# Narrower products in the last layer of a two-block transformer kernel: columns 14 to 271, and 16 to 271, in place of 0 to 271

## Chip, cores and metric

The kernel runs on one core of one Trainium2 chip. The metric is the device time of one launch in microseconds (us), the median of several runs. Inputs and outputs are float32.

## What is computed

The reference runs a first block (two layers on 256 latent tokens, with 256 context tokens beside them in the first layer) and feeds its output to a second block. The change touches the second block alone:

```python
N_META, DEPTH, CONV_W, PAD = 16, 2, 3, 128
h = concat([zeros(PAD - N_META), meta, x])          # 112 empty rows, 16 meta tokens, 256 tokens
for li in range(DEPTH):
    h = h + mixer(rms_norm(h, norm_mix_g[li]), ...)
    h = h + conv_ffn(rms_norm(h, norm_ffn_g[li]), ...)
h = rms_norm(h, norm_final_g)
return h[:, PAD:]                                   # the meta tokens are not returned

def mixer(hn, ...):
    proj = hn @ w_in                                # 13 groups of 1024 columns
    o_ret, o_hg, o_da = retention(...), hgrn2(...), diff_attention(...)   # mix tokens; two of them end in "* silu(gate)"
    y_b = [o @ w_branch[n] for n, o in enumerate((o_ret, o_hg, o_da))]
    return sum(sigmoid(mg[n]) * y_b[n]) @ w_out

def conv_ffn(hn, ...):
    u = hn @ w_ffn_in                               # width 5632
    c = conv_b + sum(conv_w[j] * up[:, j:j + l] for j in range(CONV_W))   # token t reads t-2, t-1, t
    gate, val = split(c); return (silu(gate) * val) @ w_ffn_out
```

The kernel holds the 16 meta tokens and the 256 tokens as columns 0 to 15 and 16 to 271 (`T2` = 272). The 112 empty rows are never computed. After the last layer's mixers have read keys and values of every token, no returned value depends on columns 0 to 13 any more. Columns 14 and 15 are read once more by the convolution of column 16.

## The kernel before

Everything is laid out feature-major: 128 features on the partitions, tokens along the free axis. Each product of activations with a weight matrix is done in float32 accuracy by three products of rounded parts (type float32r): high weight by high activation, high weight by low activation, low weight by high activation. They are lines 1861, 1862 and 1863, in `gemm_unit` of the TensorE program.

A weight matrix is cut into **units** of 256 output columns, a unit into **chunks** of up to four blocks of 128 input features. The tiles are these:

- `raw`, `high`, `low`: four slots of one chunk each, 128x1024. SP loads a chunk into `raw` (line 1683), ScalarE rounds it to `high` (`split_high`, line 1951), VectorE subtracts to get `low` (`split_low`, line 2136).
- `NHh`, `NHl`: high and low part of the normed activations of the second block, `OH`, `OL` those of a mixer's output, `G2H`, `G2L` those of the feed-forward's hidden layer.
- `PS`: the eight PSUM banks. Unit u writes banks 0 and 1 or 2 and 3 in turn, so that one unit's results are read out while the next is multiplied.

A unit with 1024 input features is 2 chunks x 2 output tiles x 4 blocks x 3 = 48 products. A unit of the feed-forward's output matrix has 2816 input features (6 chunks) and 22 x 2 x 3 = 132 products.

`gemm_steps` writes down the list of steps once, and every engine walks the same list. In each layer of the second block it is: stores, gate (8 or 4 units) for each of three mixers n = 0, 1, 2, then for each mixer its own attention-like part (`ret_pe`, `hg_pe`, `da_pe`), the merge gate (`mgate`, 4 units) and the branch matrix (`branch`, 4 units). Mixer 0 (retention) and mixer 1 (hgrn2) have a `gate` step of 4 units each, mixer 2 has none. Then come the output matrix (`add`, 4 units), the feed-forward's input matrix with the convolution in its epilogue (`conv`, 22 units) and its output matrix (`add` with 6 chunks, 4 units). The first two units of every `mgate` step are issued early, from within the mixer's own part, by `early_chunk` (lines 1788 to 1790) or `early_piece` (lines 1804 to 1806).

No scheduler is involved. The order on each engine is that of the program text; engines wait for each other by semaphores: `s_low` (a chunk is ready to multiply), `s_chunk` (a chunk is multiplied, its slot is free), `s_free` (a unit's banks are read out). The epilogues stand at lines 2296 to 2347 (VectorE) and 1999 to 2043 (ScalarE). For a `conv` unit they are: two scaled copies on ScalarE (line 2022), four multiply-adds of the shifted taps on VectorE (line 2331), a sigmoid on ScalarE (line 2043) and two products on VectorE (lines 2343, 2347). Each of them takes all 272 columns.

`keep_busy` issues products with a matrix of ones that nobody reads (line 529), to fill known waits of TensorE.

Of the kernel before, what the change touches and what calls it, by code (L numbers as in the profile page):

```python
# [33 lines left out]
D = 1024  # L34
KT = D // P
F = 2816
FT = F // P
SEQ = 256
CTX = 256
N_META = 16  # L40
T1 = SEQ + CTX
T2 = N_META + SEQ
DEPTH = 2
# [4 lines left out]
DEEP = ((0, 4), (4, 4), (8, 4), (12, 4), (16, 3), (19, 3))  # L48
# [96 lines left out]
    return out  # L145


def gemm_steps(w):


    steps = []

    def add(name, units, src, layer=0, t0=0, T=SEQ, kch=SHALLOW, unroll=False):
        steps.append(dict(name=name, units=units, src=src, layer=layer, t0=t0, T=T, kch=kch, unroll=unroll))

    def plain(ap, col0=0):
        v = ap.rearrange("(k p) n -> p k n", p=P)

        def src(u, k0, nk):

            n0 = (nk + 1) // 2
            return [(v[:, k0 + a:k0 + b, bass.ds(col0 + UW * u, UW)], slice(a, b), slice(0, UW))
                    for a, b in ((0, n0), (n0, nk))]
        return src

    def paired(ap, first, second):

        v = ap.rearrange("(k p) n -> p k n", p=P)

        def src(u, k0, nk):  # L170
            return [(v[:, k0:k0 + nk, bass.ds(at + P * u, P)], slice(0, nk), slice(x * P, (x + 1) * P))
                    for x, at in enumerate((first, second))]
        return src

    for layer in range(DEPTH):
        for r in range(3):
            T = T1 if (layer, r) == (0, 0) else SEQ
            if r != 1:
                half = 0 if r == 0 else 1
                add("glu", FT, paired(w["ffn_w_in"][layer, half], 0, F), layer, T=T, unroll=(layer, r) == (0, 0))  # L180
                add("res", 4, plain(w["ffn_w_out"][layer, half]), layer, T=T, kch=DEEP)
                steps[-1]["r"] = r
            elif layer == 0:
                add("v", 4, plain(w["na_w_qkv"][0], 2 * D), layer, T=T1)
                add("k", 4, plain(w["na_w_qkv"][0], D), layer, T=T1)
                steps[-1]["pairs"], steps[-1]["halves"] = {1: 0, 2: 1, 3: 2}, {u: u for u in range(4)}
                add("q", 4, plain(w["na_w_qkv"][0], 0), layer)
                steps[-1]["pairs"], steps[-1]["halves"] = {u: 3 + u for u in range(4)}, {u: 4 + u for u in range(4)}
                add("res", 4, plain(w["na_w_out"][0]), layer)
                steps[-1]["r"] = r  # L190
            else:
                add("cgate", 8, paired(w["sc_w_in"][0], D, 2 * D), layer)
                add("bgate", 4, plain(w["sc_w_in"][0], 0), layer)
                add("res", 4, plain(w["sc_w_out"][0]), layer)
                steps[-1]["r"] = r
            steps[-1]["norm"] = True
    for layer in range(DEPTH):
        w_in = w["w_in_2"][layer]
        for n, kinds in enumerate(((("store", 4, 0, 0), ("store", 4, 1024, 8), ("gate", 4, 2048, 16)),
                                   (("store", 4, 3072, 0), ("forget", 4, 4096, 8), ("store", 4, 5120, 24),  # L200
                                    ("gate", 4, 6144, 32)),
                                   (("store", 4, 9216, 16), ("store", 8, 7168, 0)))):
            for kind, units, at, tile in kinds:
                add(kind, units, plain(w_in, at), layer, T=T2, unroll=True)
                steps[-1]["tile"] = tile
                steps[-1]["at"] = at
                steps[-1]["after_rms"] = at == 0
                steps[-1]["rope"] = {0: {1: (0, 1), 2: (2, 3), 3: (4, 5)}, 1024: {0: (6, 7)},
                                     7168: {u: (2 * u - 2, 2 * u - 1) for u in range(1, 8)}}.get(at, {})
                steps[-1]["values"] = {2048: 0, 6144: 1, 7168: 2}.get(at)  # L210
            steps[-1]["mixer"] = n
            add("mgate", 4, plain(w_in, 10240 + n * D), layer, T=T2)
            steps[-1]["n"] = n
            steps[-1]["begun"] = 2
            add("branch", 4, plain(w["w_branch_2"][layer, n]), layer, T=T2)
            steps[-1]["n"] = n
        add("add", 4, plain(w["w_out_2"][layer]), layer, T=T2)
        steps[-1]["rms"] = ("ffn_g", layer)
        add("conv", FT, paired(w["w_ffn_in_2"][layer], 0, F), layer, T=T2)
        steps[-1]["after_rms"] = True  # L220
        add("add", 4, plain(w["w_ffn_out_2"][layer]), layer, T=T2, kch=DEEP)
        steps[-1]["rms"] = ("mix_g", layer + 1) if layer + 1 < DEPTH else ("final_g", 0)
    U, S = 0, 0
    for s in steps:
        s["U0"], s["S0"] = U, S
        U += s["units"]
        S += s["units"] * len(s["kch"])
    return steps, S
# [23 lines left out]
def two_block_kernel(nc, w, tokens, meta, cols_d, const1_d, const2_d, rpb_d, rpb_skew, out_d):  # L252
    steps, n_chunks = gemm_steps(w)
    ctx = ExitStack()
    with ctx:
# [89 lines left out]
        NHh = B.take("NHh", [P, KT, T2], F32R)  # L345
        nhl_at = B.at
        NHl = B.take("NHl", [P, KT, T2], F32R)
# [29 lines left out]
        PS = ctx.enter_context(nc.psum_tensor("PS", [P, 8, PW], F32))  # L377
# [139 lines left out]
        def bank(p, j, n=1):  # L517
            return PS[:, 2 * p + j:2 * p + j + n, :]
# [1210 lines left out]
        def _(pe):  # L1729
# [47 lines left out]
            def early_chunk(s, x):  # L1777

                u, c = divmod(x, 2)
                S, b = s["S0"] + x, early_bank(s["n"], u)  # L1780
                pe.wait_ge(s_low, S + 5)
                if c == 0:
                    pe.wait_ge(s_free, s["U0"] + u + (2 if s["n"] == 1 else 1))
                for j in range(2):
                    for k in range(4):
                        wh, wl = high[:, x, k, j * P:(j + 1) * P], low[:, x, k, j * P:(j + 1) * P]
                        xh, xl = NHh[:, 4 * c + k, :], NHl[:, 4 * c + k, :]
                        nc.tensor.matmul(PS[:, b + j, 0:T2], wh, xh, start=(c == 0 and k == 0), stop=False)
                        nc.tensor.matmul(PS[:, b + j, 0:T2], wh, xl, start=False, stop=False)
                        last = nc.tensor.matmul(PS[:, b + j, 0:T2], wl, xh, start=False, stop=(c == 1 and k == 3))  # L1790
                last.then_inc(s_chunk, 1)

            def early_piece(s, i):

                f, c = divmod(i, 2)
                u, j = divmod(f, 2)
                x = 2 * u + c
                pe.wait_ge(s_low, s["S0"] + x + 5)
                if c == 0 and f:
                    pe.wait_ge(s_fill, 4 * s["layer"] + f)  # L1800
                for k in range(4):
                    wh, wl = high[:, x, k, j * P:(j + 1) * P], low[:, x, k, j * P:(j + 1) * P]
                    xh, xl = NHh[:, 4 * c + k, :], NHl[:, 4 * c + k, :]
                    nc.tensor.matmul(PS[:, 6, 0:T2], wh, xh, start=(c == 0 and k == 0), stop=False)  # L1804
                    nc.tensor.matmul(PS[:, 6, 0:T2], wh, xl, start=False, stop=False)  # L1805
                    last = nc.tensor.matmul(PS[:, 6, 0:T2], wl, xh, start=False, stop=(c == 1 and k == 3))  # L1806
                if j:
                    last.then_inc(s_chunk, 1)
                elif c:
                    last.then_inc(s_filled, 1)  # L1810

            for n_step, s in enumerate(steps):
                name, T, t0 = s["name"], s["T"], s["t0"]
# [3 lines left out]
                if name in ("glu", "q", "k", "v", "cgate"):  # L1817
                    mh, ml = XH, XL
                elif name == "res":
                    mh, ml = (XH, XL) if (s["layer"] == 0 and s["r"] == 1) else (GH, GL)  # L1820
                elif name in ("store", "gate", "forget", "mgate", "conv"):
                    mh, ml = NHh, NHl
# [22 lines left out]
                def gemm_unit(u, p, S, slot0):  # L1845
                    kch = s["kch"]
                    for c, (k0, nk) in enumerate(kch):
# [5 lines left out]
                                pe.wait_ge(s_oln, half_first(s["layer"], 2) + 2)  # L1853
                        slot = (slot0 + c) % NSLOT
                        for j in range(2):
                            out = bank(p, j)[:, :, 0:T].rearrange("p a n -> p (a n)")
                            for k in range(nk):
                                wh = high[:, slot, k, j * P:(j + 1) * P]
                                wl = low[:, slot, k, j * P:(j + 1) * P]
                                xh, xl = mh[:, k0 + k, t0:t0 + T], ml[:, k0 + k, t0:t0 + T]  # L1860
                                nc.tensor.matmul(out, wh, xh, start=(k0 + k == 0), stop=False)  # L1861
                                nc.tensor.matmul(out, wh, xl, start=False, stop=False)  # L1862
                                last = nc.tensor.matmul(out, wl, xh, start=False,  # L1863
                                                        stop=(c == len(kch) - 1 and k == nk - 1))
# [704 lines left out]
```

## Time and profile before

| | us |
|---|---|
| median of 3 runs | 3172.04 (3171.92 to 3173.32) |
| the profiled execution, its own time | 3167.65 |
| span of its records | 3165.8 |
| last layer of the second block, within the span | about 2342 to 3166 |
| TensorE busy, share of the span | 95% |
| VectorE, ScalarE, GpSimd busy | 54%, 42%, 13% |
| mean granted TensorE clock | 0.976 |

The profile gives the start of each TensorE instruction exactly and models its end, so a product of 272 columns shows as 0.29 us although the next starts 0.126 us after it. The distance from start to start is therefore what a product costs in a dense stretch. In a window of the view by stretches, the count of TensorE includes the two products that still run when the window opens; the distance is the window's length divided by the count less 2.

### The profile page before, as it was taken

What the parts mean: (1) busy time and instruction counts of PE and PEld (TensorE: products, weight loads), DVE (VectorE), ACT (ScalarE), POOL (GpSimd) and SP (SyncE); (2) the same over time, 40 slices, a digit from 0 to 9 for tenths busy, and PEclk for the clock granted to TensorE, in tenths of its full rate; (3) what the DMA queues carried; (4) which work ended last, traced back from release to release, by engine and by line L of the source; (5) the groups of instructions that cost most, each with busy time, mean ns of one, the idle gap of its engine ahead of it and who ended that gap; (6) DMA issues with size and microseconds to landing.
All of it is one profiled execution on the core that took longest, in us unless ns stands there. A gap on an engine that the chain in (4) does not pass through costs nothing. (4 is left out here: it accounts for less than half of the span.)

```text
span 3165.8 us, 54076 instructions
## 1 busy us (share of the span) xinstructions
PE 2992.5 (95%) x21052; PEld 2702.8 (85%) x21052; DVE 1713.8 (54%) x2476; ACT 1341.5 (42%) x1838; POOL 408.5 (13%) x306
## 2 busy tenths in 40 slices
PE   5999998988999999999999999899999998999998
PEld 2667765666999999899899889799999997988998
DVE  2223324365555556555545755657754576565784
ACT  1222213135544434443454443556544453445563
POOL 2111000122111210121100210101110012020110
PEclk8999999999999999999999989999999998999999
DMA  8986354731555654465445315245543540533553
GB/s 295 282 251 185 121 160 125 218 95 54 160 181 148 182 180 149 143 180 181 134 127 164 110 40 174 81 134 152 173 154 120 167 153 14 161 93 116 147 172 124
DMA packets 586161, 474.88 MB, mean 150 GB/s; under 512 B 28720, under 2 KB 547888, under 8 KB 585664
## 3 DMA queue, kind: packets, MB, share of 16 engines
q1 hardware_dynamic: 584464, 460.44, 47.6%
q0 software_dynamic: 1520, 11.95, 1.2%
q8 instruction: 127, 2.08, 0.3%
q14 instruction: 50, 0.41, 0.0%
HBM read 471.23 MB, written 4.72 MB: 150 GB/s over the span
## 5 line engine op out<-in xcount | busy, mean ns | idle before, releaser
L2136 DVE TENSOR_TENSOR low<-raw,high 128x1024 fp32r<-128x1024 f32 (+1 forms) x744 | 913.1, 1231 | 837.3 <-ACT high L1951 829.2
L1951 ACT CAST high<-raw 128x1024 fp32r<-128x1024 f32 (+1 forms) x744 | 767.9, 1033 | 1102.3 <-PE PS L1863 807.6
L1861 PE MATMUL PS<-NHh,high 128*128 128x272 f32 x2304 | 672.9, 292 | 12.4 <-issue 4.7
L1863 PE MATMUL PS<-NHh,low 128*128 128x272 f32 x2304 | 666.2, 289 | 0.0
L1862 PE MATMUL PS<-NHl,high 128*128 128x272 f32 x2304 | 664.4, 288 | 0.0
L1861 PE MATMUL PS<-XH,high 128*128 128x256 f32 (+1 forms) x1856 | 587.4, 316 | 28.4 <-issue 14.4
L1862 PE MATMUL PS<-XL,high 128*128 128x256 f32 (+1 forms) x1856 | 579.4, 312 | 0.0
L1863 PE MATMUL PS<-XH,low 128*128 128x256 f32 (+1 forms) x1856 | 579.1, 312 | 0.0
L1861 PEld LDWEIGHTS PS<-NHh,high 128*128 128x128 f32 x2304 | 433.8, 188 | 17.2 <-issue 14.8
L1862 PEld LDWEIGHTS PS<-NHl,high 128*128 128x128 f32 x2304 | 434.0, 188 | 0.8
L1863 PEld LDWEIGHTS PS<-NHh,low 128*128 128x128 f32 x2304 | 433.5, 188 | 0.0
L1861 PEld LDWEIGHTS PS<-XH,high 128*128 128x128 f32 x1856 | 356.7, 192 | 79.1 <-issue 58.9
L1863 PEld LDWEIGHTS PS<-XH,low 128*128 128x128 f32 x1856 | 356.5, 192 | 20.1
L1862 PEld LDWEIGHTS PS<-XL,high 128*128 128x128 f32 x1856 | 356.8, 192 | 17.8
L1861 PE MATMUL PS<-GH,high 128*128 128x256 f32 (+1 forms) x768 | 238.8, 311 | 0.8 <-POOL GL L2461 0.8
L1863 PE MATMUL PS<-GH,low 128*128 128x256 f32 (+1 forms) x768 | 236.2, 308 | 0.0
L1862 PE MATMUL PS<-GL,high 128*128 128x256 f32 (+1 forms) x768 | 236.1, 307 | 0.0
L2461 POOL TENSOR_TENSOR GL<-SG,GH 128x256 f32 (+1 forms) x92 | 122.3, 1329 | 722.8 <-ACT GH L2036 628.8
L1861 PEld LDWEIGHTS PS<-GH,high 128*128 128x128 f32 x768 | 146.6, 191 | 26.4 <-issue 20.3
L1863 PEld LDWEIGHTS PS<-GH,low 128*128 128x128 f32 x768 | 146.7, 191 | 7.2
L1862 PEld LDWEIGHTS PS<-GL,high 128*128 128x128 f32 x768 | 146.7, 191 | 6.2
L2353 DVE TENSOR_TENSOR SG<-SG,PS 128x256 f32<-128x256 f32 (+1 forms) x88 | 42.9, 487 | 155.7 <-ACT SG L1999 155.7
(315 smaller groups left out, 4109.3 us busy)
## 6 DMA issues: line engine op xcount, KB each, us to landing
raw<-w_in_dram SPq DMA_DIRECT2D x416, 256.0 KB, 3.0
raw<-ffn_w_in_dram SPq DMA_DIRECT2D x352, 256.0 KB, 3.2
part<-ada_w_dram SPq DMA_DIRECT2D x184, 256.0 KB, 3.9
raw<-w_ffn_in_dram SPq DMA_DIRECT2D x176, 256.0 KB, 3.2
raw<-ffn_w_out_dram SPq DMA_DIRECT2D x160, 256.0 KB, 3.1
raw<-w_branch_dram SPq DMA_DIRECT2D x96, 256.0 KB, 3.3
raw<-w_ffn_out_dram SPq DMA_DIRECT2D x80, 256.0 KB, 3.0
part_sg<-ada_w_dram SPq DMA_DIRECT2D x48, 256.0 KB, 3.0
```

The lines of the kernel that those rows point to most:

```text
L1861: nc.tensor.matmul(out, wh, xh, start=(k0 + k == 0), stop=False)
L1862: nc.tensor.matmul(out, wh, xl, start=False, stop=False)
L1863: last = nc.tensor.matmul(out, wl, xh, start=False, stop=(c == len(kch) - 1 and k == nk - 1))
L1951: nc.scalar.copy(high[:, slot, 0:nk, :], raw[:, slot, 0:nk, :]).then_inc(s_high, 1)
L2136: nc.vector.tensor_tensor(low[:, slot, 0:nk, :], raw[:, slot, 0:nk, :], high[:, slot, 0:nk, :].bitcast(F32), ALU.subtract).then_inc(s_low, 1)
L2353: nc.vector.tensor_tensor(sg, sg, bank(p, 0)[:, :, 0:T], ALU.mult).then_inc(s_mid, 1)
L2461: nc.gpsimd.tensor_tensor(out, x, h.bitcast(F32), ALU.subtract).then_inc(s_hl, 1)
```

## The change

The column range of a step, `t0` to `T`, existed but `t0` was always 0. Now `needed(layer)` gives 0 for the first layer of the second block and 14 (`N_META - 2`) for the last. The steps `gate`, `mgate`, `branch`, both `add` steps and `conv` of the last layer get it; for the second `add` (the feed-forward's output) it is 16. The moving operand and the PSUM output of their products begin at that column. Weights, loads, splits, waits and epilogues stay: the epilogues of VectorE and ScalarE still read all 272 columns of the banks, of which the first 14 or 16 now hold what an earlier product left. Each engine has the same instructions in the same order as before.

```diff
+def needed(layer):
+    return 0 if layer + 1 < DEPTH else N_META - 2
...
+                if kind == "gate":
+                    steps[-1]["t0"] = needed(layer)
...
-            add("mgate", 4, plain(w_in, 10240 + n * D), layer, T=T2)
+            add("mgate", 4, plain(w_in, 10240 + n * D), layer, t0=needed(layer), T=T2)
...
-            add("branch", 4, plain(w["w_branch_2"][layer, n]), layer, T=T2)
+            add("branch", 4, plain(w["w_branch_2"][layer, n]), layer, t0=needed(layer), T=T2)
...
-        add("add", 4, plain(w["w_out_2"][layer]), layer, T=T2)
+        add("add", 4, plain(w["w_out_2"][layer]), layer, t0=needed(layer), T=T2)
...
-        add("conv", FT, paired(w["w_ffn_in_2"][layer], 0, F), layer, T=T2)
+        add("conv", FT, paired(w["w_ffn_in_2"][layer], 0, F), layer, t0=needed(layer), T=T2)
...
-        add("add", 4, plain(w["w_ffn_out_2"][layer]), layer, T=T2, kch=DEEP)
+        add("add", 4, plain(w["w_ffn_out_2"][layer]), layer, t0=needed(layer) and N_META, T=T2, kch=DEEP)
...
-                            out = bank(p, j)[:, :, 0:T].rearrange("p a n -> p (a n)")
+                            out = bank(p, j)[:, :, t0:T].rearrange("p a n -> p (a n)")
...
-                                xh, xl = mh[:, k0 + k, t0:t0 + T], ml[:, k0 + k, t0:t0 + T]
+                                xh, xl = mh[:, k0 + k, t0:T], ml[:, k0 + k, t0:T]
```

`early_chunk` and `early_piece` get the same slices, `s["t0"]:T2`, for both operands and the output.

## Rows read from the trace of the kernel before

**Rows 1.** The page: span, TensorE, VectorE and its clock in 40 slices.

```profile
span 3165.8 us, 54076 instructions
...
PE 2992.5 (95%) x21052; PEld 2702.8 (85%) x21052; DVE 1713.8 (54%) x2476; ACT 1341.5 (42%) x1838; POOL 408.5 (13%) x306
...
PEclk8999999999999999999999989999999998999999
```

**Rows 2.** The chain that ended last, from 2940 us on: start, us, what.

```profile
2955.23 0.36 PE PS L1861
3151.76 0.73 DVE H L2321
```

**Rows 3.** Stretches: length, then PE busy (count), PEld, DVE, ACT, POOL, clock, DMA.

```profile
2958.00:3082.00 124.00, 124.00 (x985) 124.00 (x985) 101.31 (x163) 79.72 (x124) 20.98 (x20) 1.00 0.58 171
3090.00:3150.00 60.00, 60.00 (x481) 60.00 (x481) 24.86 (x25) 21.17 (x24) 6.09 (x6) 1.00 0.44 137
1130.00:1190.00 60.00, 60.00 (x502) 60.00 (x501) 28.98 (x30) 22.37 (x23) 6.19 (x6) 1.00 0.60 181
300.00:350.00 50.00, 50.00 (x222) 41.42 (x221) 16.17 (x17) 13.87 (x17) 6.93 (x5) 1.00 0.24 74
2706.30:2709.40 3.10, 3.10 (x15) 3.10 (x15) 2.83 (x3) 2.60 (x4) 0.00 (x0) 0.50 0.59 185
```

**Rows 4.** Waits of TensorE from 2342 us on: us in total, times, longest.

```profile
PE PS L1139 <- DVE AM L1363: 2.9, 1, 2.9
...
PE PS L1861 <- DVE NHl L1667: 2.3, 3, 1.5
PE PS L1861 <- DVEq L2305: 2.1, 1, 2.1
...
PE PS L1788 <- DVE MG L2300: 1.6, 1, 1.6
...
PE PS L1861 <- DVE MG L2300: 1.1, 1, 1.1
```

**Rows 5.** Timeline around the second merge gate's end: start, length, instruction, idle before.

```profile
2703.39 0.29 PE L1863 MATMUL PS<-NHh,low 128*128 128x272 f32 x1
2703.64 1.28 ACT L2008 ACT_TABLE_LOAD   x1
...
2704.93 0.62 ACT L2008 ACTIVATE GR<-PS 128x544 f32<-128x544 f32 x1
...
2705.79 0.36 PE L1861 MATMUL PS<-OH,high 128*128 128x272 f32 x1 [2.11 <-DVEq L2305]
```

**Rows 6.** Timeline of VectorE and TensorE in hgrn2's gate.

```profile
2577.05 5.03 DVE L1323 TENSOR_TENSOR_SCAN MI<-con,MI 128x272 f32<-128x272 f32 x8
...
2583.34 0.70 DVE L2300 TENSOR_TENSOR MG<-MG,PS 128x544 f32<-128x544 f32 x1
...
2584.19 0.36 PE L1861 MATMUL PS<-NHh,high 128*128 128x272 f32 x1 [1.08 <-DVE MG L2300]
```

**Rows 7.** Timeline of VectorE, one unit of the last `conv` step.

```profile
2995.71 2.19 DVE L2331 SCALAR_TENSOR_TENSOR CB<-PS,cols,CB 128x271 f32<-128x271 f32 x4 [0.62 <-ACT CB L2022]
2997.82 1.22 DVE L2136 TENSOR_TENSOR low<-raw,high 128x1024 fp32r<-128x1024 f32 x1
2998.95 0.43 DVE L2343 TENSOR_TENSOR SG<-SG,CB 128x272 f32<-128x272 f32 x1
2999.51 0.44 DVE L2347 TENSOR_TENSOR SG<-SG,CB 128x272 f32<-128x272 f32 x1
2999.87 1.22 DVE L2136 TENSOR_TENSOR low<-raw,high 128x1024 fp32r<-128x1024 f32 x1
```

**Rows 8.** Stretch of the last layer's stores of mixer 2, columns as in rows 3.

```profile
2779.00:2811.00 32.00, 32.00 (x243) 31.37 (x242) 20.82 (x34) 9.47 (x10) 11.72 (x10) 1.00 0.49 152
```

More of the change, by code:

```diff
@@ L1786, in early_chunk @@
                         wh, wl = high[:, x, k, j * P:(j + 1) * P], low[:, x, k, j * P:(j + 1) * P]
[L1787 to L1790, printed above, removed]
+                        xh, xl = NHh[:, 4 * c + k, s["t0"]:T2], NHl[:, 4 * c + k, s["t0"]:T2]
+                        out = PS[:, b + j, s["t0"]:T2]
+                        nc.tensor.matmul(out, wh, xh, start=(c == 0 and k == 0), stop=False)
+                        nc.tensor.matmul(out, wh, xl, start=False, stop=False)
+                        last = nc.tensor.matmul(out, wl, xh, start=False, stop=(c == 1 and k == 3))
                 last.then_inc(s_chunk, 1)
@@ L1802, in early_piece @@
                     wh, wl = high[:, x, k, j * P:(j + 1) * P], low[:, x, k, j * P:(j + 1) * P]
[L1803 to L1806, printed above, removed]
+                    xh, xl = NHh[:, 4 * c + k, s["t0"]:T2], NHl[:, 4 * c + k, s["t0"]:T2]
+                    out = PS[:, 6, s["t0"]:T2]
+                    nc.tensor.matmul(out, wh, xh, start=(c == 0 and k == 0), stop=False)
+                    nc.tensor.matmul(out, wh, xl, start=False, stop=False)
+                    last = nc.tensor.matmul(out, wl, xh, start=False, stop=(c == 1 and k == 3))
                 if j:
```

## The prediction
> **What bounds the kernel now.** I read the page first. TensorE is busy for 95% of a span of 3165.8 us, and its clock is full nearly everywhere [rows 1]. Busy time alone doesn't say that TensorE sets the end, since its ends are modelled. So the chain of work that ended last comes next: from 2955.23 us, where the last layer's `conv` step gets going, to 3151.76 us it is nothing but products of lines 1861 to 1863, and only then come the last addition and the final norm [rows 2]. Third come the waits of TensorE in the last layer: the largest one of a product that the change touches is 2.1 us, and all that touch such a product are in rows 4. TensorE is the bound of this layer, with short breaks inside the mixers. So what counts is what a product costs from start to start, and at which breaks a shorter product only waits longer.
>
> **The cost of a product by its width.** The view by stretches gives it, each window's length divided by its count less 2 [rows 3]. In the last `conv` step 272 columns cost 124.0 / 983 = 126.1 ns. In the feed-forward's output step, also 272 columns, they cost 60.0 / 479 = 125.3 ns. In the first block's output step of 1130 to 1190 us, 256 columns cost 60.0 / 500 = 120.0 ns. In the window at 300 us, 512 columns cost 50.0 / 220 = 227.3 ns. Between 256 and 272 a column is worth 6.1 / 16 = 0.38 ns, between 272 and 512 it is 101.2 / 240 = 0.42 ns. So the width is paid for, on top of a fixed part of some 13 ns. The changed products have 258 columns, two more than a width that the trace shows: 120.0 + 2 x 0.38 = **120.8 ns**, 5.3 ns less than before. Bounds: not below the 120.0 ns of 256 columns, and not above the 126.1 ns of today unless the new start column costs something (a rival, below). I take 120.8, since the nearest row is two columns away.
>
> The Trainium skill, "TensorE: Matmul & The Clock Gate", section on the back-to-back issue gap, has the distance at full clock as N / 2.4 + 2.5 ns. The trace differs on the fixed part (13 ns, not 2.5) and nearly agrees on the slope. By the page's slope a product saves 14 / 2.4 = 5.8 ns, and the sum below would be 18.7 us instead of 16.6.
>
> **The change, part by part.** Products of 258 columns: `gate` 8 units, `mgate` 12, `branch` 12, the output matrix 4, `conv` 22, together 58 units of 48, or 2784 products. Products of 256 columns: 4 units of 132, or 528.
>
> *conv, 1056 products.* The stretch is dense for all of its 124 us [rows 3]. What must keep up is VectorE: in one unit, 2995.71 to the last row's end, it has 2.19 + 1.22 + 0.43 + 0.44 + 1.22 = 5.50 us of work, with some overlap, and before it 0.62 us of idle time that ended with a ScalarE result [rows 7]. A unit now takes 48 x 126.1 = 6.05 us and will take 5.80 us. VectorE's idle time shrinks from 0.62 to about 0.37 us and stays above nothing. Its result is needed only when the unit after next begins, so a delay of a few tenths is covered by a whole unit. DMA is busy at 0.58 and the 256-wide stretch ran at 0.60 [rows 3], so loads can follow. Full gain: 1056 x 5.3 = 5.6 us.
>
> *Feed-forward output, 528 products.* Dense too, VectorE busy 24.9 of 60 us [rows 3]. 125.3 - 120.0 = 5.3 ns each: 2.8 us, all on the chain [rows 2].
>
> *The other 1728 products.* Most stand back to back with TensorE's next work. At two places the gain is swallowed:
> - The second merge gate's units 2 and 3 (96 products) end at 2703.4, and the branch product starts only at 2705.79, when a sigmoid of ScalarE (2704.93) is out. That one stood behind a table load and the casts of the mixer's output, none of which waits for those 96 [rows 5]. Shorter products lengthen this wait: gain nothing.
> - In hgrn2's gate, VectorE spends 2577.05 to 2583.34 on the running sums and only then frees the banks of unit 0; TensorE waits for it until 2584.19 [rows 6]. Units 0 and 1 (96 products) end earlier for nothing, but for a little of unit 0 that lets VectorE begin sooner. I count nothing.
>
> The rest keeps its gain. The waits for `L2300` before an early piece and for `L1363` after it [rows 4] follow the end of products and move with them; those for `L1667` come after the norm, and move as well. The third merge gate is followed by no wait in rows 4. So 1728 - 192 = 1536 products x 5.3 = 8.1 us.
>
> Half clock: 2706.3 to 2709.4 ran at 0.50 (1.2 of 2.4 GHz), after the break before it, and held 15 products [rows 3, 5]. At half clock 14 columns are worth twice as much, 13 x 5.8 = 0.1 us more. The break before it gets 0.5 us longer, so this stretch stays.
>
> Nothing is removed on VectorE, ScalarE, GpSimd, SP or the DMA queues, so nothing else is gained.
>
> **Sum:** 5.6 + 8.1 + 0.1 + 2.8 = **16.6 us**. The profiled execution took 3167.65 us by its own time (span 3165.8), 4.4 us under the median of 3172.04. The sum is a difference within that execution, and I take it off both: 3151.0 for such an execution, **3155.4 us** for the median, a gain of 0.5%.
>
> **Rivals.**
>
> *B. The start at column 14 takes back what the width gives.* Columns 0, 16 or 128 begin at a multiple of 64 bytes in their row, column 14 at byte 56, and the touched 258 columns reach into as many 64-byte pieces (17) as the 272 did. All widths in rows 3 start at column 0, so no row shows an uneven start. If reads go by such pieces, only the 528 products from column 16 gain: 2.8 us, 3169.2. Against it: nothing seen, only lack of a row.
>
> *C. The weight load sets most of the pace.* Every product has a load of its own. The 256 to 512 rows speak against it, with 0.38 and 0.42 ns a column [rows 3]. As a mechanism here, 258 would be near a floor, and the gain would be small: at a third of the slope, 2592 x 1.8 + 528 x 2.1 = 5.8 us, 3166.2. The Trainium skill, same page and section, gives for pairs of load and product 81 ns at 128 columns and 131 ns at 512, a slope of 0.13 ns; by this rule the time would be that of C, but the trace's 227.3 ns at 512 contradicts it.
>
> *D. Another engine holds the `conv` step.* If VectorE and ScalarE, which still take 272 columns, kept the unit at 6.05 us, the 5.6 us of `conv` would be lost: 11.0 us gained, 3161.0. For it: 5.50 us of work in 5.80. Against it: the 0.62 us of idle time, and a whole unit of cover [rows 7].
>
> *E. Slower: the uneven start makes reading slower.* Place: the moving operand and the PSUM output of 2592 products. It outweighs the 2.8 us of the feed-forward's output from 1.1 ns a product above today's 126.1, and costs 0.2% from 3.5 ns. The nearest dearer row at full clock is the stores' stretch, 32.0 / 241 = 132.8 ns, other work and small breaks included [rows 8]. At that price it is 2592 x 6.7 - 2.8 = 14.6 us slower, 3186.6. For it there is only that no row shows column 14; against it, that a read of fewer columns would have to cost more than a read of all.
>
> That the change doesn't do what it says can be left out: the diff narrows each product, and count and order stay.
>
> **How the numbers follow.** A (the forecast) 0.80, B 0.07, C 0.03, D 0.06, E 0.04. Within A: at 120.0 ns and with the 192 swallowed products counted, 2784 x 6.1 + 2.8 = 19.8 us; at a price halfway to today's, 2592 x 3.05 + 2.8 = 10.7 us. A stretch of half clock more or less costs some 1.4 us (15 products counted in 3.1 us where full clock holds 3.1 / 0.126 + 2 = 26.6) [rows 3]. A's own range is thus 3151 to 3162. With D inside and 1 us for a half-clock stretch at either end, **3150 to 3163**; it leaves out B, C, E and the tails of A. A measurement of this kernel can tell about 0.2% (6.3 us) from no change. Faster: A and D, 0.86. Within: B and C, 0.10. Slower: E, 0.04.
>
> **What would show it.** In the changed profile: the `conv` window shows about 120.8 ns a product and no wait on VectorE or ScalarE; the feed-forward's output shows 120.0. The wait before the second branch product grows from 2.1 to about 2.6 us, that in hgrn2's gate from 1.1 to about 1.6. The last addition of the page's chain starts about 16.6 us sooner. The forecast is wrong if the 258-column products show 126 ns or more (B, E) while those from column 16 show 120, if both barely move (C), or if a wait of a microsecond appears in the `conv` step (D).

## The result, and the profile after

The changed kernel takes 3147.35 us (median of 6 runs, 3140.8 to 3151.08), the kernel before 3172.68 us in the same comparison (3170.8 to 3173.86). The ratio is 0.9921, with a 95% interval of 0.9912 to 0.9931: 25.1 us less, between 21.9 and 27.9. The forecast was 16.6 us less, with a range that ended at 3150 us. So direction and place were right, and the gain was half as large again as forecast.

The page of the changed kernel, with its execution of 3140.8 us:

```profile
span 3139.0 us, 54076 instructions
...
PE 2966.2 (94%) x21052; PEld 2677.4 (85%) x21052; DVE 1714.8 (55%) x2476; ACT 1343.3 (43%) x1838; POOL 408.3 (13%) x306
...
PEclk8999999999999999999999989999999999999999
```

TensorE is busy 26.3 us less than in [rows 1], VectorE as long as before. Lines are 7 to 9 higher than before: 1861 to 1863 are now 1870 to 1872. The chain that ended last, from 2915 us on (start, us, what), has the same links as in [rows 2]:

```profile
2938.93 0.36 PE PS L1870
3124.94 0.73 DVE H L2330
```

The cost of a product comes from the same view as in [rows 3], columns as there, the window's length divided by the count less 2:

```profile
2945.00:3060.00 115.00, 115.00 (x963) 115.00 (x962) 99.54 (x161) 76.82 (x121) 21.02 (x20) 1.00 0.62 181
3065.00:3122.00 57.00, 57.00 (x486) 57.00 (x485) 26.89 (x28) 21.64 (x25) 6.11 (x6) 1.00 0.47 150
2467.00:2488.00 21.00, 21.00 (x179) 21.00 (x178) 11.39 (x11) 8.17 (x8) 0.00 (x0) 1.00 0.62 190
1125.00:1185.00 60.00, 60.00 (x502) 60.00 (x502) 29.84 (x31) 22.33 (x24) 6.59 (x6) 1.00 0.60 183
```

That is 115.0 / 961 = 119.7 ns in the `conv` step, 57.0 / 484 = 117.8 ns in the feed-forward's output, 118.6 ns in the first branch step (118.9 as the mean of its start distances), and still 120.0 ns for 256 columns in the first block. The forecast had 120.8, 120.0 and 120.8 for the first three. The same width of 256 columns thus costs 120.0 ns in one place and 117.8 in another. That is what the experiments are about.

Where the time went, by the first and last start of each step in both traces: from the last layer's first product to the end of the span it was 817.1 us and is 793.8, so 23.3 us less. The `conv` step has 6.6 of it (133.65 to 127.06), the feed-forward's output 3.9 (65.98 to 62.07), everything else in the layer 12.8. Another 3.6 us of the 26.8 between these two spans had come before the layer began, where nothing was changed; that part is chance.

The waits of TensorE from 2338 us on (us in total, times, longest):

```profile
PE PS L1870 <- DVE NHl L1674: 2.4, 3, 1.5
...
PE PS L1870 <- DVEq L2314: 2.3, 1, 2.3
...
PE PS L1796 <- DVE MG L2309: 1.6, 1, 1.6
PE PS L1870 <- DVE MG L2309: 1.5, 1, 1.5
```

They answer to [rows 4]. The wait before the second branch product grew from 2.1 to 2.3 us and the one in hgrn2's gate from 1.08 to 1.54; the other two moved by no more than 0.1. The timeline of hgrn2's gate, start and length, shows the second one, as in [rows 6]:

```profile
2575.58 0.71 DVE L2309 TENSOR_TENSOR MG<-MG,PS 128x544 f32<-128x544 f32 x1
...
2576.43 0.36 PE L1870 MATMUL PS<-NHh,high 128*128 128x258 f32 x1 [1.54 <-DVE MG L2309]
```

One stretch of half clock is gone. It had lain at the start of the second branch step, whose 192 products run from 2705.79 to 2731.45 us in the kernel before (first fence) and from 2696.32 to 2719.26 us in the changed one (second fence; columns as in [rows 3]):

```profile
2705.79:2731.45 25.66, 25.66 (x191) 25.66 (x192) 16.23 (x16) 10.46 (x11) 0.00 (x0) 0.93 0.67 205
```

```profile
2696.32:2719.26 22.94, 22.94 (x192) 22.94 (x192) 16.16 (x16) 10.47 (x11) 0.00 (x0) 1.00 0.71 218
```

The step is 2.7 us shorter, of which the width explains 192 x 6.4 ns = 1.2 us (126.1 to 119.7 ns in this step) and the clock, 1.00 in place of 0.93, the other 1.5.

### The profile page after: what moved, and what is told of

It is laid out like the page before. It is cut to its first block and busy times, and to the rows that moved or that the text cites. A ratio compares the mean times of both kernels' runs of the same rounds, so it can differ in the third digit from the quotient of the medians.

```text
span 3139.0 us, 54076 instructions
## 1 busy us (share of the span) xinstructions
PE 2966.2 (94%) x21052; PEld 2677.4 (85%) x21052; DVE 1714.8 (55%) x2476; ACT 1343.3 (43%) x1838; POOL 408.3 (13%) x306
## 5 line engine op out<-in xcount | busy, mean ns | idle before, releaser
L1870 PE MATMUL PS<-NHh,high 128*128 128x272 f32 (+1 forms) x2304 | 669.0, 290 | 13.1 <-DVE NHl L1674 4.7
L1872 PE MATMUL PS<-NHh,low 128*128 128x272 f32 (+1 forms) x2304 | 661.5, 287 | 0.0
L1871 PE MATMUL PS<-NHl,high 128*128 128x272 f32 (+1 forms) x2304 | 660.2, 287 | 0.0
```

The costliest lines, as they stand in the source:

```text
L1872: last = nc.tensor.matmul(out, wl, xh, start=False, stop=(c == len(kch) - 1 and k == nk - 1))
```

## The experiments

All start from the changed kernel unless said otherwise. Ratios are to the kernel before. The runs from column 0, with the table of widths and with 128 columns leave out columns that the result needs; they measure cost alone.

**Start column or width?** Operands and outputs of the same widths, but from column 0:

```diff
-                            out = bank(p, j)[:, :, t0:T].rearrange("p a n -> p (a n)")
+                            out = bank(p, j)[:, :, 0:T - t0].rearrange("p a n -> p (a n)")
-                                xh, xl = mh[:, k0 + k, t0:T], ml[:, k0 + k, t0:T]
+                                xh, xl = mh[:, k0 + k, 0:T - t0], ml[:, k0 + k, 0:T - t0]
```

The same slices stand in `early_chunk` and `early_piece`.

> Same widths as the change, but from column 0: products read and write columns 0 to 257 (0 to 255 in the feed-forward's output), so the last columns of the last layer are left out. In the changed kernel a product of 258 columns cost 118.9 ns (119.7 in the conv step) and one of 256 columns 117.8 ns, not the forecast 120.8 and 120.0. Theory W (the width alone, with a fixed part of some 11 ns wherever tiles lie 1088 bytes apart): the same distances within 0.5 ns, and a time within 3 us of the change's 3147. Rival S (the start at byte 56 or 64 of a row is what makes products cheaper): 258 columns come back to 120.8, 256 to 120.0, time about 3155.

Measured: 3148.86 us, ratio 0.9927 (0.9910 to 0.9943). `conv` had 115.0 / 960 = 119.8 ns, the feed-forward's output 58.0 / 492 = 117.9 ns, the three branch steps 119.7 ns. With column 14 those had 118.9, 119.7 and 118.9. So the width does nearly all, and the uneven start costs nothing. Whether it gives the 0.8 ns in two of the steps is not shown: with column 14 the same step had 118.9 in one run and 119.7 in another. Rival S fell.

**Where the row starts.** All tiles of the first block 64 bytes later:

```diff
-        A = Region(common_end)
+        A = Region(common_end + 64)
```

> The changed kernel with all tiles of the first block (XH, XL, GH, GL and what lies behind) moved by 64 bytes; rows of XH still lie 2048 bytes apart. Before, every 256-column product of the first block was exactly 120.0 ns from the next. Theory R (what matters is that successive operands start at the same place within 256 bytes as each other): still 120.0 ns. Rival L (what matters is where the operand starts relative to the weight slots, which start 128 bytes past a multiple of 256, as all tiles of the first block do): another distance than 120.0 ns, by 1 ns or more.

Measured, by the view of stretches:

```profile
1110.00:1160.00 50.00, 50.00 (x427) 50.00 (x426) 25.78 (x29) 21.61 (x27) 6.08 (x6) 1.00 0.57 178
```

50.0 / 425 = 117.6 ns (117.8 by the mean of all distances of such products), where it had been 120.0 without exception. 512 columns went from 228.0 to 229.2, by the mean of the distances in dense stretches, as all prices of 512 columns below. One execution took 3140.46 us. Nothing but an address had changed. This is what my sum lacked.

**Another row pitch** for XH and XL, `[P, KT, T1 + 16]` in place of `[P, KT, T1]`:

> The changed kernel with XH and XL given 528 columns a row in place of 512, so that rows start 2112 bytes apart as 64 more than a multiple of 256; widths unchanged. Theory P (the fixed part of a product is smaller where successive rows start at different places within 256 bytes): the 256-column products from XH and XL fall from 120.0 to about 117.8 ns, those from GH and GL stay at 120.0; 4128 products x 2.2 = 9 us less than the change. Rival (the row pitch has no part in it): 120.0 stays, no gain.

Measured: 3136.62 us, ratio 0.9898 (0.9880 to 0.9916), 7 us less than the change's by the ratios (0.0023 of 3172.7). The 256-column products from XH and XL stood mostly at 118.3 ns, those from GH and GL at 120.0. Theory P predicted the direction; the value was 0.5 ns off.

**Two more places**, `common_end + 128` and `+ 192`:

> The changed kernel with the first block's tiles moved by 128 bytes, so that rows of XH, XL, GH and GL start at a multiple of 256 bytes, 128 away from the weight slots. Moving by 64 bytes took a 256-column product from 120.0 to 117.75 ns and a 512-column one from 228.0 to 229.2. Theory L (the distance depends on the place of the moving row relative to that of the weight slot within 256 bytes): a third pair of values, neither 120.0 nor 117.75. Rival (only equal starts cost 2.3 ns extra): 117.75 again.

> As f3, moved by 192 bytes. Theory L: a fourth pair of values; the mean over the four places should be near the 117.8 ns that the 256-column products of the feed-forward's output show, whose rows take all four places in turn. Rival (only equal starts cost extra): 117.75.

Measured: at 128 bytes 118.7 ns in most stretches and 120.0 in some, and 232.5 for 512 columns (one execution, 3151.89 us). At 192 bytes one execution took 3124.84 us:

```profile
1110.00:1160.00 50.00, 50.00 (x443) 50.00 (x442) 26.13 (x29) 20.89 (x25) 7.79 (x6) 1.00 0.60 194
```

50.0 / 441 = 113.4 ns for 256 columns, but 233.4 for 512. The four places give 120.0, 117.8, 118.7 and 113.3 ns. Their mean is 117.5; the feed-forward's output, whose rows lie 1088 bytes apart and so take all four places in turn, shows 117.8. Product by product the two don't match, though: in that step of the changed kernel the mean distance behind a product of high weight and high activation is 120.5, 115.0, 119.7 and 119.2 ns with the row at 0, 64, 128 and 192 bytes. So the price of a row among rows at other places can't be read from a stage where all rows have its place, and the near agreement of the means may be chance.

**Relative to what?** The weight slots 64 bytes later, the activation tiles where they were:

```diff
+        R.take("pad", [P, 16])
         high = R.take("high", [P, NSLOT, 4, UW], F32R)
...
-        small = R.take("small", [P, 40 * KT])
+        small = R.take("small", [P, 38 * KT])
```

> The changed kernel with the weight slots (high, low) moved by 64 bytes and the activation tiles left where they were; all tiles of the first block are then 64 bytes behind the slots, which is the same distance within 256 bytes as being 192 ahead. Theory L (what counts is the place of the moving row relative to the weight slot): the values of the run moved by 192 bytes, 113.3 or 117.8 ns for 256 columns and 233 for 512, in place of 120.0 and 228.0. Rival (what counts is the moving tile's own address): 120.0 and 228.0, as in the change. A stretch keeps one of the two values until TensorE pauses, so a mean between them says only which share ran at which.

Measured: 3127.73 us, ratio 0.9866 (0.9844 to 0.9889).

```profile
1110.00:1160.00 50.00, 50.00 (x427) 50.00 (x426) 27.57 (x30) 20.85 (x27) 7.35 (x7) 1.00 0.58 182
1400.00:1450.00 50.00, 50.00 (x443) 50.00 (x443) 28.33 (x33) 23.01 (x32) 8.77 (x7) 1.00 0.63 191
```

117.6 ns in the one window, 113.4 in the other, and 233.4 for 512 columns: the values of the place at 192 bytes, though no activation tile of the first block had moved. What counts is where the moving row starts relative to the weight slot; for the places at 64 and 128 bytes this was not tried from the weights' side. Theory L held, its rival fell.

**The same kernel as f4, timed in rounds:**

> The kernel of f4 again, timed in rounds. One execution took 3124.84 us. Theory L by the distances: 5904 x 5.9 - 1806 x 5.4 = 25 us less than the change, about 3122; ratio to the kernel before about 0.984.

Measured: 3132.97 us (3123.15 to 3140.23), ratio 0.9879 (0.9859 to 0.9900), 11 us above the forecast. The trace, of an execution of 3126.05 us, says why in part:

```profile
1110.00:1160.00 50.00, 50.00 (x427) 50.00 (x426) 26.56 (x30) 21.90 (x29) 6.56 (x6) 1.00 0.57 180
...
1400.00:1450.00 50.00, 50.00 (x444) 50.00 (x443) 27.87 (x34) 24.32 (x33) 8.89 (x8) 1.00 0.60 185
```

The first window has 117.6 ns, where the same kernel had 113.4 in the run before; the second has 113.1. At this place a product has two prices, 113.3 and 117.8. In the four traces with 256 columns at this place (f4, g3, g1, h1) a stretch keeps one of them, over up to 1584 products, and it changes only where TensorE had paused. At 128 bytes there are two as well, 118.7 and 120.0.

**Both widths at their best place.** The 256-column stages of the first block use columns 48 to 303 of their rows, the 512-column stages still start at 0:

```diff
+LATE = 48
+def cs(T):
+    return slice(LATE, LATE + T) if T == SEQ else slice(0, T)
...
-                    nc.scalar.copy(XH[:, k:k + 2, 0:T], TQ[:, k:k + 2, 0:T]).then_inc(s_xh, 1)
+                    nc.scalar.copy(XH[:, k:k + 2, cs(T)], TQ[:, k:k + 2, 0:T]).then_inc(s_xh, 1)
```

and so wherever XH, XL, GH and GL are written or read; the sum of rows that lay in the same place moves to the free columns behind them.

> The changed kernel; in the first block the stages with 256 columns keep XH, XL, GH and GL in columns 48 to 303 of their 512-column rows, so that they start 192 bytes later, while the 512-column stages stay at column 0. Moving all tiles by 192 bytes gave 114.1 ns for 256 columns (120.0 before) but 233.4 ns for 512 (228.0 before). Theory L: 114.1 and 228.0 together; 5904 products x 5.9 = 35 us less than the change, about 3112, ratio to the kernel before about 0.981. Rival (something else of that run made it fast): 120.0 stays.

Measured: 3122.47 us (3112.57 to 3125.74), ratio **0.9838** (0.9818 to 0.9859). 512 columns cost 228.0 ns, and 256 columns 117.8 in most stretches, 113.3 in a few. It beats both kernels, by 1.6% the one before and by some 25 us the change, though not by the 35 us forecast. In the trace some 770 of the 5904 products of 256 columns had the lower price; its time lies 18.3 us under that of the changed kernel's trace (3122.47 and 3140.8), and these products make 770 x 6.4 + 5134 x 2.2 ns = 16.2 us of that (113.6 and 117.8 in place of 120.0 ns). The medians lie 25 us apart; the executions between them have no trace.

**How far does width go?** A table of widths in one run:

```diff
-                    steps[-1]["t0"] = needed(layer)
+                    steps[-1]["t0"] = layer and (8, 12)[n]
...
-            add("mgate", ..., t0=needed(layer), T=T2)
+            add("mgate", ..., t0=layer and (32, 24, 144)[n], T=T2)
-            add("branch", ..., t0=needed(layer), T=T2)
+            add("branch", ..., t0=layer and (16, 64, 80)[n], T=T2)
```

with a start at column 112 for the output matrix (160 columns) and 16 for `conv`.

> A table of widths in one run, by steps of the last layer, all ending at column 271 (columns are left out, so the output is not complete): gates 264 and 260, merge gates 240, 248 and 128, branches 256, 208 and 192, output matrix 160, conv 256, feed-forward output 256. Theory (0.42 ns a column plus 11 to 13 ns, down to a floor set by the weight load): 264: 123, 260: 120, 256: 117.8, 248: 114, 240: 111, 208 and less: a floor; the load of 128 columns lasts at least 107 ns if it runs at half the clock of the columns. Rival (120.0 ns is a floor): 240 columns and fewer stay at 118 to 120.

Measured, the windows in the order 240, 256, 192, 160 and 256 (`conv`) columns:

```profile
2466.00:2475.80 9.80, 9.80 (x89) 9.80 (x89) 7.48 (x9) 5.94 (x8) 0.00 (x0) 1.00 0.60 172
2477.00:2498.00 21.00, 21.00 (x181) 21.00 (x180) 11.42 (x11) 8.25 (x8) 0.00 (x0) 1.00 0.65 197
2911.00:2931.00 20.00, 20.00 (x182) 20.00 (x181) 14.04 (x15) 7.81 (x8) 0.00 (x0) 1.00 0.72 228
2937.00:2956.00 19.00, 19.00 (x173) 19.00 (x171) 9.88 (x10) 9.02 (x10) 5.29 (x5) 1.00 0.50 145
2972.00:3090.00 118.00, 118.00 (x1000) 118.00 (x999) 102.07 (x166) 79.58 (x124) 21.06 (x20) 1.00 0.61 180
```

The mean distances of the steps are 121.7 ns at 264 columns, 119.4 at 260, 118.2 at 256, 115.6 at 248, 112.2 at 240, and 111.7 at 208, 192, 160 and 128 alike (128 in the third merge gate's units 2 and 3). So there is a floor of 111.7 ns, reached near 240 columns, and between 240 and 272 a column is worth (126.1 - 112.2) / 32 = 0.43 ns. 120.0 is no floor. The surprise was the whole: with fewer columns than the change this run took 3170.73 us, 30 us longer.

**Why it was slower.** One width of that table alone:

```diff
-            add("mgate", ..., t0=needed(layer), T=T2)
+            add("mgate", ..., t0=144 if layer and n == 2 else needed(layer), T=T2)
```

> The changed kernel with the third merge gate of the last layer narrowed further, to columns 144 to 271 (128 of them; the rest of that gate is left out). In the run with a table of widths TensorE's clock stayed at half from 2823 to 2895 us, where the first two units of this gate are issued in pieces between the attention's own products. Theory H (the shorter pieces leave TensorE less active there, and its clock falls and stays down): again a half-clock stretch of some tens of us from about 2805 on, and an execution 15 to 30 us longer than the change's. Rival (it was another of the narrowed steps, or chance): half-clock stretches of 10 us as in the change, and some 2 us shorter than the change.

Measured: 3163.35 us, one execution. In the first fence the kernel with 128 columns, in the second the changed one, in the same part of the program:

```profile
2810.00:2882.00 72.00, 68.84 (x298) 56.11 (x299) 31.52 (x141) 32.25 (x112) 0.00 (x0) 0.50 0.10 30
```

```profile
2803.00:2880.00 77.00, 70.94 (x478) 58.30 (x479) 45.09 (x169) 51.20 (x138) 2.00 (x3) 0.87 0.18 55
```

TensorE's granted clock was 0.50, 1.2 of 2.4 GHz, for 71.7 us without a break; the run with the table of widths has a stretch of the same length there. Before it fell, TensorE had waited for the last rotated keys, as in every run; then the short pieces of the merge gate stood between the attention's small products. In the changed kernel two half-clock stretches of 10.2 us lie there, in the kernel before 3.4 and 13.7. From the first of those pieces to unit 2 of that gate it took 72.4 us in place of 51.2: 21 us more, with 96 shorter products in it. Theory H held, in one execution of each kernel.

**Parts of the change.** Only `conv` and the feed-forward's output narrowed, the other steps back at 272 columns:

> Only the last conv step (258 columns) and the feed-forward's output (256 columns) are narrowed; gates, merge gates, branches and output matrix of the last layer have 272 columns again. Theory (every product that stands back to back keeps its whole saving): conv 1056 x 6.3 = 6.6 us and output 528 x 7.4 = 3.9 us, together 10.5 us, ratio to the kernel before about 0.9967, and no other step of the last layer shorter. Rival D of the prediction (conv is held by VectorE or ScalarE): under 7 us.

Measured: ratio 0.9960 (0.9946 to 0.9974), 12.7 us less, between 8.2 and 17.1. In the trace `conv` took 127.1 us and the output 62.1, as in the change: 10.5 us. The rest of the layer had the distances of before. Rival D fell.

Only the products that I had counted at nothing (units 0 and 1 of hgrn2's gate, units 2 and 3 of the second merge gate), all others of the last layer at 272 columns:

```diff
+                    t0 = 0
+                    if s["layer"] == 1 and (name == "mgate" and s["n"] == 1 or name == "gate" and s["tile"] == 32 and u < 2):
+                        t0 = needed(1)
```

> Only products that the prediction counted at nothing are narrowed: units 0 and 1 of hgrn2's gate and units 2 and 3 of the second merge gate (its units 0 and 1 too, but they are issued early and keep 258 columns: 96 more that count). All else in the last layer has 272 columns. Theory (the two waits grow by what the products save): about 0.7 us from the early units and 0.1 to 0.5 us from the rest, ratio within 0.9995 to 1.0000 but for chance. Rival (they all count): 288 x 7 ns = 2.0 us.

Measured: ratio 1.0005 (0.9995 to 1.0014), no gain. In the trace the second merge gate's unit 2 to the first branch product took 14.46 us (14.48 before), hgrn2's gate to the next step 29.70 us (29.87 before). The expectation is wrong in one point: the early units of that merge gate had 272 columns in this run, as in the kernel before, and so 192 products were narrowed, not 288. What the early ones give shows in the changed kernel: from the first of them to unit 2 it was 92.35 us and is 91.70, so those 96 keep their whole gain, 0.65 us.

## Why the prediction was right and wrong

- **TensorE sets the end of the last layer.** Right. The chain, the dense stretches and the absence of new waits of size all stayed.
- **The price of a narrow product.** Wrong, and this is the step that failed: "120.0 + 2 x 0.38 = 120.8 ns", with the bound "not below the 120.0 ns of 256 columns". The row with 120.0 came from tiles of another layout. Its rows all start at the same place, within 256 bytes, as the weight slots, and this is the dearest of the four places at that width. In the second block rows take all places in turn. There 258 columns cost 118.9 to 119.7 ns and 256 columns 117.8. That place and row pitch make the 120.0 is shown (117.8 after a move of 64 bytes, 118.3 with another pitch); how 117.8 and 118.9 come about from the single rows is open. One number in [rows 3] should have warned me: 120.0 was exact for hundreds of products, while 272 columns gave 126.1 in one tile and 125.3 in another, at equal width.
- **The terms.** `conv` gained 6.6 us for a forecast of 5.6, the feed-forward's output 3.9 for 2.8. The other 1536 products, at 6.4 to 7.2 ns (126.1 less 119.7 to 118.9), give some 10.7 us for a forecast of 8.1. With them the sum is 21.2 us; the layer's 23.3 us hold 2.1 more: some 0.6 us in the two places that I had counted at nothing, and 1.5 us of the half-clock stretch that is gone. So the right price alone would have made the forecast 3150.8 us. The rest of the measured 25.1 us had no term in my sum: the stretch of half clock, and what executions differ by.
- **Two places swallow their gain.** Right in kind: alone, these products changed nothing that the times could tell, and both waits grew. The one in hgrn2's gate grew by 0.46 us, as forecast (0.5), the one before the second branch product by 0.2, so that of the second merge gate's gain 0.4 us came through.
- **VectorE keeps up in `conv`.** Right: 119.7 ns a product, and one wait of 0.44 us at the step's second chunk.
- **Rivals.** B and E (the uneven start takes or costs time) fell with the run from column 0. C (near a floor already) fell at these widths, but there is a floor 7 ns below them; that the weight load makes it is not shown. D fell. The Trainium skill's slope of 1 / 2.4 ns a column (TensorE: Matmul & The Clock Gate, the section cited in the prediction) would have given 5.8 ns a product, nearer to the measured 7.2 but also short; from 272 to 258 a column was worth 0.51 ns in the branch steps.
- **Half clock.** "So this stretch stays" was wrong for the trace of the changed kernel, where the one at 2706.3 us is gone (1.5 us); in the run from column 0, equal in width, it is there (clock 0.93 over a branch step of 24.46 us). Nothing in the runs says which comes when. I allowed one stretch more or less, 1.4 us, but the changed kernel's own runs lie 10 us apart. At full speed, too, the `conv` step had 119.7 ns in some traces and 110.0 / 926 = 118.8 ns in another with the same last layer (f4), so the price itself varies from run to run.

## What to carry to other kernels

A price read from another stage holds only with that stage's addresses: take the distance from start to start for each tile and row pitch, and where it is exact to the nanosecond over a whole stage, suspect an alignment and not the width. Where TensorE is the bound, moving the activation tiles against the weight slots is an edit of a line or two. By ratios to the kernel before, 192 bytes took the change's 0.9921 to 0.9879, and moving the weight slots by 64 took it to 0.9866, 13 and 17 us; 128 bytes gained nothing (3151.89 us, one execution). Each width has its own best place, so try all four. Below a floor narrower products save nothing, and where they stand between small products they can cost the clock.

## What the runs showed of the hardware

- The distance of successive products depends on where the moving row starts relative to the weight slot, within 256 bytes. For 256 columns it was 120.0 ns at equal places, 117.8 at 64 bytes, 118.7 or 120.0 at 128, and 113.3 or 117.8 at 192. For 512 columns it was 228.0, 229.2, 232.5 and 233.4: the order is another one. Why is open; with all rows at one place, only steps of 64 bytes were tried.
- At some places there are two prices. A stretch keeps one until TensorE pauses. What picks it was not found. That it makes the times of one kernel differ is not shown: those of the best kernel lie 13 us apart (3112.57 to 3125.74), but those of the kernel before, whose 256-column products cost 120.0 ns throughout its trace, 9 us (3164.58 to 3173.95). Between the traces of the changed kernel and of the run from column 0, 6.3 of 8.0 us had arisen by 755 us, in code that is the same in both: from 640 to 770 us the granted clock was 0.95 in the one and 0.89 in the other.
- A product with its own weight load cost 111.7 ns at 208, 192, 160 and 128 columns alike.
- With 128-column products between the attention's small ones, TensorE counted as busy for 68.8 of 72 us and ran at half clock all that time (granted clock 0.50).
